# Where the gate operand begins in SBUF: the start of two arrays modulo 512 bytes in a two-block float32 transformer kernel

## The reference, cut to what matters

```python
# first_block, last lines of a layer
h = h + 0.5 * _swiglu_ffn(_rms_norm(h, ffn2_norm[i]), ffn2_w_gate_up[i], ffn2_w_down[i])
e = _rms_norm(p[i] @ w_ple[i], ple_norm[i])
h = h + jax.nn.sigmoid(h @ w_ple_gate[i]) * e

# second_block, last lines of a layer
h = h + conv_ffn(rmsnorm(h, ln_ffn[i]), w_up[i], ffn_conv[i], w_down[i])
gate = jax.nn.sigmoid(rmsnorm(h, ln_ple[i]) @ w_ple_gate[i])
h = h + gate * rmsnorm(p[i] @ w_ple[i], ple_norm[i])
```

## Time and profile before

| What | Value |
|---|---|
| time of three runs | 3951.73, 3953.51, 3958.05 us |
| median | 3953.51 us |
| span of the profiled execution | 3950.6 us |
| median less that span | 2.9 us |
| TensorE matmul busy | 3812.4 us, 97% |
| TensorE weight load busy | 3050.4 us, 77% |
| VectorE busy | 2334.5 us, 59% |
| ScalarE busy | 1510.9 us, 38% |
| GpSimd busy | 511.5 us, 13% |
| mean granted TensorE clock | 0.986 |

### The profile page before, as it was taken

One profiled execution on the slowest core, in us unless ns is written; L12 is line 12 of the kernel. 1 busy time (PEld: TensorE's weight loads), 2 busy tenths in 40 slices (PEclk: granted clock), 3 DMA queues, 4 the chain that ended last, 5 costly groups with the idle time before them and its releaser, 6 DMA issues. The chain is left out here.

```text
span 3950.6 us, 46607 instructions
## 1 busy us (share of the span) xinstructions
PE 3812.4 (97%) x17790; PEld 3050.4 (77%) x17790; DVE 2334.5 (59%) x3213; ACT 1510.9 (38%) x2188; POOL 511.5 (13%) x366
## 2 busy tenths in 40 slices
PE   8999989999999998999989999999999999999997
PEld 6888758888788885788877678788877767878886
DVE  5455766445544475744467675775567665675656
ACT  3224653223322365322243444343343353343333
POOL 1001731000100055100020013200010002220002
PEclk9999989999999999999999999999999999999999
DMA  4333203333233330233332100122233110022222
GB/s 152 96 96 112 66 21 96 96 96 111 86 98 99 97 106 11 79 100 96 96 114 80 49 22 1 43 96 96 96 109 107 59 38 6 12 80 96 96 96 80
DMA packets 87018, 314.99 MB, mean 80 GB/s; under 512 B 10016, under 2 KB 10400, under 8 KB 86176
## 3 DMA queue, kind: packets, MB, share of 16 engines
q1 hardware_dynamic: 83664, 302.43, 24.4%
q10 hardware_dynamic: 3152, 9.74, 0.7%
HBM read 307.94 MB, written 2.10 MB: 78 GB/s over the span
## 5 line engine op out<-in xcount | busy, mean ns | idle before, releaser
L384 ACT ACTIVATE wh<-raw 128x1024 fp32r<-128x1024 f32 x564 | 597.4, 1059 | 1630.3 <-PE ps L404 1317.5
L402 PE MATMUL ps<-xh,wh 128*128 128x512 f32 x2336 | 918.0, 393 | 16.7 <-DVE xl L467 10.0
L403 PE MATMUL ps<-xl,wh 128*128 128x512 f32 x2336 | 910.8, 390 | 0.0
L404 PE MATMUL ps<-xh,wl 128*128 128x512 f32 x2336 | 910.5, 390 | 0.0
L388 DVE TENSOR_TENSOR wl<-raw,wh 128x1024 fp32r<-128x1024 f32 x564 | 695.6, 1233 | 181.1 <-ACT wh L384 180.2
L402 PEld LDWEIGHTS ps<-xh,wh 128*128 128x128 f32 x2336 | 439.8, 188 | 112.4 <-issue 19.6
L403 PEld LDWEIGHTS ps<-xl,wh 128*128 128x128 f32 x2336 | 440.0, 188 | 94.3 <-issue 3.6
L404 PEld LDWEIGHTS ps<-xh,wl 128*128 128x128 f32 x2336 | 439.8, 188 | 91.9
L402 PE MATMUL ps<-fh,wh 128*128 128x512 f32 x1016 | 397.1, 391 | 4.0 <-DVE wl L388 4.0
L404 PE MATMUL ps<-fh,wl 128*128 128x512 f32 x1016 | 395.4, 389 | 0.0
L403 PE MATMUL ps<-fl,wh 128*128 128x512 f32 x1016 | 395.3, 389 | 0.0
(11 more groups left out here) (467 smaller groups left out, 5529.6 us busy)
## 6 DMA issues: line engine op xcount, KB each, us to landing
raw<-in_w SPq DMA_DIRECT2D x564, 512.0 KB, 3.5
con<-in_consts SPq DMA_DIRECT2D x1, 2053.5 KB, 14.0
h<-in_x SPq DMA_DIRECT2D x4, 512.0 KB, 6.9
p_t<-in_p ACTq DMA_DIRECT2D x4, 512.0 KB, 3.9
w1k<-in_w1c ACTq DMA_DIRECT2D x2, 1024.0 KB, 4.9
w1v<-in_w1c ACTq DMA_DIRECT2D x2, 1024.0 KB, 7.0
out<-h SPq DMA_DIRECT2D x8, 256.0 KB, 2.2
dup_k<-roped ACTq DMA_DIRECT2D x8, 128.0 KB, 3.6
```

The lines of the kernel that those rows point to most:

```text
L384: nc.scalar.activation(wh[k % 2][:, :], raw[k % 4][:, :], ACT.Copy).then_inc(s["w_hi"], 1)
L402: nc.tensor.matmul(DB[k % 2][:, :], a, hi(q), start=(q == order[0]), stop=False)
L403: nc.tensor.matmul(DB[k % 2][:, :], a, lo(q), start=False, stop=False)
L404: last = nc.tensor.matmul(DB[k % 2][:, :], b, hi(q), start=False, stop=(q == order[-1]))
```

## The change

The gate operand gets its own small shift. Where its layout began right behind the small parameters, it now begins at the next offset that equals `x_at` modulo 512. `x_at` is 128 modulo 512, so `gate1hi` moves from 186368 to 186496 and `gate1lo` from 202752 to 202880 (128 bytes up), and `gate2hi` moves from 185088 to 185472 and `gate2lo` from 201472 to 201856 (384 bytes up). All four now are 128 modulo 512. The layout `m` of the other buffers is not moved, since `gl_` is a layout of its own. `gate2lo` now ends at 218240 and reaches 352 bytes into `state` (217888 to 218400), a buffer of the mixing part, which is done with before the gate operand is written.

```diff
@@ -26,6 +26,7 @@
 GROUPS = [8, 8, FC - 16]
 AHEAD = 3
 UW = DC * P
+LINE = 512
 FFN_UNITS = sum(2 * g + DC for g in GROUPS)
@@ -652,7 +653,7 @@
                 m = Layout(nc, mix_at, sb.end - mix_at)
                 small = small1
                 m.at += -(-4 * NS1 // 32) * 32
-                gl_ = Layout(nc, m.at, 32768)
+                gl_ = Layout(nc, m.at + (x_at - m.at) % LINE, 32768)
                 gh, gl = (gl_(f"gate1{n}", [P, DC, T], F32R) for n in ("hi", "lo"))
```

## The result

The changed kernel takes 3961.95 us (median of 20 runs, 3957.65 to 3965.29), the kernel before 3953.27 us (20 runs, 3951.68 to 3958.05). The ratio is 1.0020, with a 95% interval of 1.0013 to 1.0027: slower by 0.2%. Forecast was 3948.6 us, with a range up to 3955.5. The profiled execution of the changed kernel took 3962.51 us, 1.8 us more than its span. So of the 2.9 us that were taken as lying around the span of before, 1.1 us are likely spread between executions; the forecast starts from the median and is not touched by it.

The account below looks back on a forecast made before the run. TensorE's matmuls were taken as the bound, busy 3812.4 of 3950.6 us. Gain 5.12 - 0.20 = 4.9 us, other terms nothing, so 3953.5 - 4.9 = 3948.6 us; range 3943.5 to 3955.5 us.

Parts of the forecast that it names:

- Reads by TensorE: Four gate stages: 768 matmuls reading the moved arrays each lose 6.67 ns, a gain of 5.12 us.
- the statistics matmul: Block 2's two gate stages: it already waits for GpSimd's sum, so 0.10 us is lost in each, 0.20 us together.
- The first rival: Gate matmuls: distance or part of memory, not the start, costs the 6.67 ns; nothing changes, 3953.5 us; chance 0.14.
- Writes: Writes of the gate arrays: the new start costs the writing engines nothing that shows; counted as nothing, at most 0.13 us.
- VectorE in the third stage: Third gate stage: VectorE could do a unit in 5.42 us against TensorE's 5.44, so it still fits; nothing counted.
- The ends of the layers: After the last gate matmul: following work keeps the gain; low-clock shifts counted as nothing, bounds 6 us gained to 8.4 lost.
- the slower rival: Three layer ends: restart falls fully into the low-clock stretch, 2.8 us more each, 3957.0 us; chance 0.05.
- the clock's part: Three layer ends: an earlier end can meet half-clock stretches elsewhere, to either side; taken as nothing.
- moves with it and keeps the gain: Layer ends: work up to the next layer's first matmul starts from the last gate product, so none of the gain is lost.

Follow-up runs that it names:

- e7: Changed kernel with the weight and work buffers moved up 128 bytes, to 256 modulo 512, gate arrays not moved; 4033.12 us (one run).
- e11: Changed kernel with 4 (layer 0) and 3 (layer 1) more idle matmuls just ahead of block 2's mixing part; 3951.24 us, 0.9994 of the kernel before.
- e1: Kernel before with only block 1's gate arrays moved to 128 modulo 512; 3958.41 us, 1.0010 of the kernel before.
- e2: Kernel before with only block 2's gate arrays moved to 128 modulo 512; 3955.25 us, 1.0001 of the kernel before.
- e6: Changed kernel, two full-height idle matmuls behind each 64-row step of block 2's first two heads, 8 fewer idle ones later; 3963.14 us.
- e9: Changed kernel, two full-height idle matmuls behind each 64-row step of block 2's first three heads, 8 fewer idle ones later; 3964.80 us.
- e10: Kernel before, two full-height idle matmuls behind each 64-row step of block 2's first three heads, 8 fewer idle ones later; 3966.86 us.
- e8: Changed kernel with one gate array of each block at 256 modulo 512 (gate1lo, gate2hi), the other at 128; 3960.34 us (one run).
- e13: Changed kernel with its whole SBUF layout moved up 64 bytes, moving operands and weights all at 192 modulo 512; 3960.52 us (one run).
- e5: Changed kernel with 10 more idle matmuls just ahead of block 2's mixing part; 3965.93 us, 1.0028 of the kernel before.
- e3: Changed kernel with 7 idle matmuls after the second unit of each layer of block 2; 3968.20 us, 1.0032 of the kernel before.
- e4: Kernel before with 23 idle matmuls after the second unit of each layer of block 2; 3969.55 us, 1.0036 of the kernel before.

## Why the prediction was wrong, point by point

- *Reads by TensorE, 5.12 us*: right in size. The step fell from 233.3 to 226.7 ns in all four stages, and the stages are 4.8 us shorter in all, where 4.9 were forecast with the statistics matmul. The first rival (distance or part of the memory) is refuted by that, since the arrays still lie high up, and by e7, where `xh` and `fh`, low down, pay too. The Trainium skill says in "SBUF — State Buffer", "Who interferes with whom", that the two read ports of TensorE are independent and that it never waits on anyone. That the place of the arrays therefore costs nothing, as the prediction read it, is not what the runs show: with the weights 128 bytes further up, e7 took 4033.12 us, about 71 more than the changed kernel.
- *Writes, nothing*: right; ScalarE and VectorE are busy for 1511.2 and 2333.8 us, before 1510.9 and 2334.5.
- *VectorE in the third stage, 0.02 us of room*: right. Its wait for TensorE of 0.18 us is gone from the timeline, its period is 5.44 us (2981.25 to 2986.69), and TensorE has no gap:

```profile
2981.25 0.69 DVE L2930 TENSOR_TENSOR gbuf<-ps,rstd 128x512 f32<-128x512 f32 x1
2982.40 1.23 DVE L389 TENSOR_TENSOR wl<-raw,wh 128x1024 fp32r<-128x1024 f32 x1 [0.46 <-ACT wh L385]
...
2986.69 0.69 DVE L2930 TENSOR_TENSOR ubuf<-ps,rstd 128x512 f32<-128x512 f32 x1
```

- *The statistics matmul takes back 0.10 us each*: right within 0.02 us in the third stage, where its wait grew from 0.49 to 0.57 us.

```profile
2956.24 0.30 PEld L481 LDWEIGHTS ps<-rstd,con 128*128 128x128 f32 x2 [0.57 <-POOL rstd L447]
```

- *The ends of the layers*: the term taken as nothing was 1.9 us in the profiled pair, 0.6 to 0.7 us at each of three ends, within the bounds given. It is not what made the kernel slower: the slower rival needed over 4.9 us there.
- *The step that failed*: the clock's part, a term taken as nothing, was looked for at the layer ends alone. The low stretches behind them were read. The other eight inside the layers of the kernel before were left out of the sum without a reason: six in block 1 (504 to 579 and 1521 to 1596 us) and two in the mixing part of block 2 (2412.2 and 3350.8 us). In the last two TensorE is busy all along at half clock, which would have told that the clock also falls while it works, and so that a shift of the work can cost in the middle of a layer. In the mixing part of block 2 11.8 us were lost in the profiled pair. The argument "moves with it and keeps the gain" holds for the order of the instructions and not for the clock they run at. By the medians, e11 against the changed kernel, the whole of what the clock took and the pad gave back is 12.3 us. Busy time by stretch, the kernel before, one low stretch in the first layer and one in the third:

```profile
504.10:514.40 10.30, 8.78 (x30) 6.99 (x31) 3.01 (x8) 5.85 (x21) 4.88 (x4) 0.50 0.01 2
2412.20:2419.00 6.80, 6.80 (x26) 5.61 (x26) 2.81 (x5) 1.84 (x3) 0.00 (x0) 0.50 0.00 0
```

- *The slower rival* was right in kind (a shift of the work against the low stretches) and wrong in place, and its chance of 0.05 and its price of 8.4 us at most were too small.

Shown, by e1, e2 and e11: the same change is a loss or not by where it brings the mixing part, and seven idle matmuls ahead of it undo the loss. Shown by e6, e9 and e10: what stands in the head's row matters too. Not settled: why the clock falls there at all; where exactly the good place ends (273.0 us is out in e8 and e13, 273.6 in; 274.2 is in, 274.8 out in e5) and whether it is met in every run, since each kernel has one profile; and whether e11 really beats the kernel before: it should be 3.3 us faster by its own sum (4.9 less 1.57) and measured 1.9, with an interval that holds 1.

## What to carry to other kernels

Let operands that move through TensorE and the weights they meet begin at the same place modulo 512 bytes, and not at a multiple of 256, since the runs don't part these two rules; here it is worth 3% of each dense matmul. Before costing a small gain in a TensorE-bound kernel, list all stretches at half clock in its trace, those inside busy parts above all, and ask whether the shift moves such a place: a gain of 5 us was turned into a loss of 9, and a pad of 1.6 us took the loss away. Test a shift by a delay put where TensorE waits for nothing, and take its length from the trace.

## What the runs showed of the hardware

- Float32r matmuls of 128x128 by 128x512 follow each other after 226.7 ns in the mean when moving operand and weights begin at the same place modulo 512 (both at 128 in the changed kernel, both at 192 in e13), and after 233.3 ns (operand at 0 or 256, weights at 128, the kernel before) or 232.4 ns (operand at 128, weights at 256, e7) otherwise. In all slow cases one of the two is at a multiple of 256.
- The granted clock fell to half while TensorE was busy without a gap, within or right behind 4 us in which most matmuls use 64 of 128 rows (2338.2 us in the changed kernel, 2412.2 in the kernel before). With two more full-height ones behind each step it stayed at 1.00 there (e6, 2332.9 to 2350.0 us).
- A float32 matmul of 128x128 shows as two records: 7 more of them are 14 records and 1.48 us in e3, 23 are 46 and 5.05 us in e4.
- The time from the clock's rise at the start of block 2 to the first such row is the same to 0.1 us in profiles of kernels with the same work between (272.6 us in the changed kernel, e6 and e9, 273.6 and 273.7 in e2 and the kernel before). That it repeats from run to run of one kernel is not profiled, but the loss does: all 20 runs of the changed kernel took 3957.65 us or more, and 14 of the 20 of the kernel before 3953.61 or less.
